# Expert rows read back in two parts, and the end of a streaming encoder layer put in another order

## The reference, cut to what matters

```python
def hier_moe(h, w_group, b_group, w_er, b_er, w_gate, w_up, w_down):
    ...
    p_top, g_top = lax.top_k(jax.nn.softmax(g_logits, -1), 1)
    ...
    e_val, e_top = lax.top_k(e_logits, TOP_E)            # TOP_E = 2 of the group's 8 experts
    gate = jax.nn.softmax(e_val, -1) * p_top
    expert = g_top * EXPERTS_PER_GROUP + e_top            # one of 32
    ...
        hid = jax.nn.silu(xb @ w_gate[e]) * (xb @ w_up[e])   # 1024 -> 256
        return hid @ w_down[e]                               # 256 -> 1024
    ...
    out = out.astype(jnp.float32) * buf_w[:, None]
    return jnp.zeros((n, d), jnp.float32).at[buf_tok].add(out)

x = x + hier_moe(rmsnorm(x, g_ffn), ...)
y = rmsnorm(x, g_final)
```

## Time and profile before

| what | value |
|---|---|
| time, median of 3 executions | 1193.99 us (1193.21 to 1194.16) |
| the profiled execution's own time | 1192.71 us |
| its span, first to last instruction | 1190.9 us |
| mean granted TensorE clock | 0.992 |
| PE, DVE, ACT, POOL busy | 94%, 51%, 40%, 15% |
| HBM read and written | 177.85 MB and 30.18 MB |

### The profile page before, as it was taken

The page is one execution under the profiler, slowest core; times in us unless marked ns, Lnnn a source line. Parts: engine busy times, 40 slices in busy tenths (PEclk is TensorE's granted clock), DMA queues, the critical chain, the costliest instruction groups (busy, mean ns, idle before and its releaser), DMA issues.

```text
span 1190.9 us, 20137 instructions
## 1 busy us (share of the span) xinstructions
PE 1119.6 (94%) x7781; PEld 802.2 (67%) x7781; DVE 607.6 (51%) x1613; ACT 480.7 (40%) x1037; POOL 176.4 (15%) x268
## 2 busy tenths in 40 slices
PE   6997799999999899999999899999899999999986
PEld 5984478787878798898988678887733333333352
DVE  6528978888888785733333373355411112121126
ACT  6437668687878524244343462221011111111113
POOL 1320023434343300000000000000112121111002
PEclk9999999999999999999999999999999999999998
DMA  8343140402112043142442444202899999999748
GB/s 288 48 88 64 36 102 1 106 11 69 48 33 59 19 118 114 53 128 72 119 121 80 151 168 171 92 37 75 338 382 383 420 418 420 418 420 415 304 176 337
DMA packets 127251, 205.44 MB, mean 173 GB/s; under 512 B 15109, under 2 KB 100389, under 8 KB 114869
## 3 DMA queue, kind: packets, MB, share of 16 engines
q1 hardware_dynamic: 114868, 177.63, 42.2%
q0 software_dynamic: 10560, 21.02, 5.2%
q10 hardware_dynamic: 1728, 5.51, 1.2%
HBM read 177.85 MB, written 30.18 MB: 175 GB/s over the span
## 4 chain that ended last, share of the span: by engine, by line
PE 75%; DVE 12%; DMA 4%; ACT 4%; issue 3%; SPq 1%; POOL 0%; DVEq 0%; POOLq 0%; ACTq 0%
PE psum L2512 14%; PE psum L2527 7%; PE psum L2231 5%; PE psum L2233 5%; PE psum L2232 5%; DVE place L1471 3%; PE psum L2382 3%; PE psum L2203 3%; PE psum L2384 2%; PE psum L2383 2%; PE psum L2204 2%; PE psum L2205 2%; PE psum L2313 2%; PE psum L2479 2%; DMA place<-expert_out 2%
## 5 line engine op out<-in xcount | busy, mean ns | idle before, releaser
L2512 PE MATMUL psum<-place,place 128*32 128x512 f32 x1536 | 169.8, 594 | 1.7 <-issue 0.9
L1123 ACT ACTIVATE place<-place,place 128x768 uint8<-128x768 f32 (+3 forms) x128 | 125.5, 983 | 6.7 <-DVE place L1502 6.7
L2231 PE MATMUL psum<-place,place 128*128 128x512 f32 x288 | 121.9, 423 | 2.4 <-DVE place L1459 2.4
L2512 PEld LDWEIGHTS psum<-place,place 128*32 128x32 f32 x1536 | 48.7, 110 | 104.0 <-issue 101.4
L2233 PE MATMUL psum<-place,place 128*128 128x512 f32 x288 | 113.4, 394 | 0.0
L2232 PE MATMUL psum<-place,place 128*128 128x512 f32 x288 | 112.5, 391 | 0.0
L1917 DVE TENSOR_TENSOR place<-psum,place 128x256 f32<-128x256 f32 x24 | 10.2, 427 | 154.6 <-ACT place L1303 154.6
L2527 PE MATMUL psum<-place,place 128*32 128x512 f32 x768 | 86.9, 592 | 0.7 <-DVE place L1911 0.7
L2203 PE MATMUL psum<-place,place 128*128 128x256 f32 x288 | 85.6, 297 | 1.6 <-ACT place L1145 1.6
L2204 PE MATMUL psum<-place,place 128*128 128x256 f32 x288 | 82.1, 285 | 0.0
L2205 PE MATMUL psum<-place,place 128*128 128x256 f32 x288 | 82.0, 285 | 0.0
(11 more groups left out here) (306 smaller groups left out, 2435.9 us busy)
## 6 DMA issues: line engine op xcount, KB each, us to landing
place<-in_w_gate SPq DMA_DIRECT2D x32, 1024.0 KB
place<-in_w_up SPq DMA_DIRECT2D x32, 1024.0 KB
place<-in_w_down SPq DMA_DIRECT2D x32, 1024.0 KB
place<-in_w_in SPq DMA_DIRECT2D x28, 512.0 KB, 6.7
place<-expert_out SPq DMA_DIRECT2D x9, 1024.0 KB, 14.4
place<-in_cache_attn_k SPq DMA_DIRECT2D x32, 256.0 KB, 3.4
place<-in_cache_attn_v SPq DMA_DIRECT2D x32, 256.0 KB, 3.2
place<-in_x_prompt SPq DMA_DIRECT2D x3, 1536.0 KB, 9.4
```

Source lines behind the costliest of these rows:

```text
L1123: last = nc.scalar.activation(reached[j], score[j], ACT.Sign, bias=pivot.bitcast(F32)[:, j:j + 1], scale=-1.0, accum_out=minus[:, j - BY_A ...
L2231: nc.tensor.matmul(bank(4 + b), hT_hi[:, k, rows], hi, start=k == 0, stop=False)
L2512: last = nc.tensor.matmul(bank(b % 2)[rows], xT[b % 2][:, k, rows], w_gu[expert_of(b, q) % NSLOT][:, :, k, :], start=k == 0, stop=k == KD - 1)
```

## The change

The last three blocks (CUT = 21 to 23) are taken out of the table that the tiles are loaded from.

- Blocks 0 to 20 are scattered to expert_out as before, blocks 21 to 23 to a second table late_rows_out. SyncE fills both with zeros during retention heads 0 and 1, so that a row that a table lacks reads as zero.
- SyncE loads y_in[t] once the scatters of blocks 0 to 20 have landed, into weight buffers of experts 27 to 29 that are free by then. Some loads also wait for a block that read the buffer.
- A frame with a pick in blocks 21 to 23 is computed anew in the order of slots. Each late block has 128 slots. For them GpSimd gathers the residual rows (x1_dram, which SyncE writes), the pick's gates and the block of its other pick (pick_table, 2304 rows of 3 numbers, written by ScalarE's queue in block 0), and the other pick's result row, from the early or the late table (other_rows). VectorE adds the own pick straight from the block's rows in SBUF and the other pick. These are "tiles" 9 to 11 of the end; their rows are stored to y_p by index, after all stores of tiles 0 to 7. The sample tile is loaded by late rows on top of its early ones instead.
- Two of VectorE's tiles are summed ahead of the hidden product of block 23 and the others between its last steps. The tiles of TensorE are now 5, 6, 7 and 8. ScalarE makes the diagonal matrices in iteration 22 and takes three sums of squares before the last eviction. The roots are taken in eight groups. The stores of tiles are issued by SyncE. The idle transposes are gone.
- 12 tiles are squared, rooted, scaled and stored in place of 9.

```diff
-AWAKE_FIRST, AWAKE_ROUTE, AWAKE_LAST = (6, 9, 5), (6, 9, 9, 9, 30), 40
-ON_PE, LAST_ORDER = (1, 3, 5, 7), (0, 2, 1, 4, 3, 6, 5, 7, 8)
+CUT = NMAIN - 3
+LATE_BLOCKS = range(CUT, NMAIN)
+NLATE = len(LATE_BLOCKS)
+ON_PE = (5, 6, 7, TP)
+ON_DVE = tuple(t for t in range(T) if t not in ON_PE)
+AWAKE_FIRST, AWAKE_ROUTE = (6, 9, 5), (6, 9, 9, 9, 30)
...
+        late_rows_out = nc.dram_tensor("late_expert_out", (2 * NTOK, D), F32).ap()
...
+        x1_dram = nc.dram_tensor("residual_frames", (NTOK, D), F32).ap()
+        pick_table = nc.dram_tensor("picks", (2 * NTOK, 3), F32).ap()
...
+        LAST = list(ON_DVE) + list(ON_PE[:-1]) + LATE_ROWS + [TP]
+        ROOTS = [(0, 2), (2, 3), (3, 5), (5, 6), (6, 7), (7, 8), (8, 8 + NLATE), (8 + NLATE, 9 + NLATE)]
...
+                    empty = late_rows_out if h else expert_out
+                    sp.dma_start(empty.rearrange("(n p) d -> p n d", p=P), zeros.unsqueeze(1).broadcast_to([P, 2 * T, D])).then_inc(zeroed[0], 16)
...
+                sp.dma_start(x1_dram[t * P:(t + 1) * P, :], x1[:, t, :]).then_inc(x1_out, 16)
...
+            sp.wait_ge(y_out[0], 16 * ((CUT + 1) // 2))
+            sp.wait_ge(y_out[1], 16 * (CUT // 2))
             for t in range(T):
+                if t == 3:
+                    sp.wait_ge(gu_ps, last_block(28) + 1)
+                if t == 5:
+                    sp.wait_ge(dn_ps, last_block(28) + 1)
+                if t == 6:
+                    sp.wait_ge(gu_ps, last_block(29) + 1)
+                if t == TP:
+                    sp.wait_ge(dn_ps, last_block(29) + 1)
                 sp.dma_start(y_in[t], expert_out.rearrange("(j t p) d -> t p j d", j=2, p=P)[t]).then_inc(y_loaded(t)[0], 16)
+            y_p, y_s = o_["y_p"].rearrange("a s d -> (a s) d"), o_["y_s"].rearrange("b s d -> (b s) d")
+            for x, t in enumerate(LAST[:TP]):
+                sp.wait_ge(out_done, x + 1)
+                sp.dma_start(y_p[t * P:(t + 1) * P, :], out_rows[t]).then_inc(y7_out[x % 3], 16)
+            sp.wait_ge(out_done, T + NLATE)
+            sp.dma_start(y_s, out_rows[TP]).then_inc(y_s_out[0], 16)
...
+            pool.memset(zeros, 0.0).then_inc(pool_set, 1)
...
+            def late_frames(n):
+                b = CUT + n
+                if n == 2:
+                    pool.wait_ge(h2tr_ps, T + NMAIN)
+                pool.indirect_dma_start(late_x1[n], None, x1_dram, bass.IndirectOffsetOnAxis(ap=block_frames[:, b:b + 1], axis=0),
+                                        bounds_check=NTOK - 1, oob_is_err=False).then_inc(late_x1_in[0], 16)
+
+            def picks_of(n):
+                b = CUT + n
+                pool.indirect_dma_start(late_picks[:, n, :], None, pick_table, bass.IndirectOffsetOnAxis(ap=block_rows[:, b:b + 1], axis=0),
+                                        bounds_check=2 * NTOK - 1, oob_is_err=False).then_inc(late_picks_in[0], 16)
+
+            def other_picks(n, late):
+                pool.indirect_dma_start(other_rows[n], None, late_rows_out if late else expert_out,
+                                        bass.IndirectOffsetOnAxis(ap=late_others[:, late, n:n + 1], axis=0),
+                                        bounds_check=2 * NTOK - 1, oob_is_err=False).then_inc(others_in[0], 16)
...
+            def root(g):
+                start, end = ROOTS[g]
+                pool.wait_ge(ssq_done, 2 * T + end)
+                pool.tensor_scalar(ssq7[:, start:end], ssq7[:, start:end], 1.0 / D, EPS, ALU.mult, ALU.add).then_inc(ms_done, 1)
+                pool.wait_ge(ms_done, 2 * T + g + 1)
+                pool.tensor_tensor(rstd7[:, start:end], ssq7[:, start:end], half.broadcast_to([P, end - start]), ALU.pow).then_inc(rstd_done, 1)
...
+                if b == NMAIN:
+                    pool.wait_ge(*picks_out)
+                    pool.wait_ge(*late_cleared)
+                    pool.wait_ge(x1_out, 16 * RH + 16 * T)
+                    for n in range(NLATE):
+                        picks_of(n)
+                    late_frames(0)
+                    late_frames(1)
+                if b == NMAIN + 2:
+                    for n in range(2, NLATE):
+                        late_frames(n)
+                if b == NMAIN + 3:
+                    pool.wait_ge(*others_ready)
+                    pool.wait_ge(gu_ps, NMAIN)
+                    pool.wait_ge(y_out[0], 16 * ((CUT + 1) // 2))
+                    pool.wait_ge(y_out[1], 16 * (CUT // 2))
+                    for n in range(NLATE):
+                        other_picks(n, 0)
+                    root(0)
+                if b == NMAIN + 4:
+                    root(1)
                 if b >= 5:
                     scatter(b - 5)
...
+            root(2)
+            for m in range(2):
+                pool.wait_ge(y_out[m], 16 * (NMAIN // 2))
+            pool.wait_ge(others_in[0], 48 + 16 * NLATE)
+            for n in range(NLATE):
+                other_picks(n, 1)
+            root(3)
+            pool.wait_ge(*y_loaded(TP))
+            for j in range(2):
+                pool.indirect_dma_start(y_in[TP][:, j, :], None, late_rows_out, bass.IndirectOffsetOnAxis(ap=sample_late[:, j:j + 1], axis=0),
+                                        bounds_check=2 * NTOK - 1, oob_is_err=False).then_inc(sample_in[0], 16)
+            for g in range(4, len(ROOTS)):
+                root(g)
+            for m in range(3):
+                pool.wait_ge(y7_out[m], 16 * ((TP + 2 - m) // 3))
+            y_p = o_["y_p"].rearrange("a s d -> (a s) d")
+            for n in range(NLATE):
+                pool.wait_ge(out_done, TP + n + 1)
+                pool.indirect_dma_start(y_p, bass.IndirectOffsetOnAxis(ap=late_write[:, n:n + 1], axis=0), out_rows[T + n], None,
+                                        bounds_check=SEQ - 1, oob_is_err=False).then_inc(late_out[0], 16)
...
+                if b == 0:
+                    act.dma_start(pick_table.rearrange("(j t p) m -> p (j t) m", j=2, p=P), pick_values.rearrange("p j t m -> p (j t) m")).then_inc(picks_out[0], 16)
+                if b == NMAIN - 2:
+                    act.wait_ge(gu_ps, NMAIN - 1)
...
+                            nc.scalar.activation(gate_diagonal[n][j], ident, ACT.Copy, scale=gates[:, j, t:t + 1]).then_inc(mix_hi_done, 1)
+                if b == NMAIN - 1:
+                    act.wait_ge(gu_ps, NMAIN)
+                    square(0)
+                    square(1)
...
+            square(2)
             rows_out(NMAIN - 1)
...
+            def own_pick(n):
+                if n == 0:
+                    v.wait_ge(*late_x1_in)
+                    v.wait_ge(y_act, NMAIN)
+                    v.wait_ge(y_dve, NMAIN)
+                nc.vector.scalar_tensor_tensor(late_x1[n], y_of(CUT + n), late_picks[:, n, 0:1], late_x1[n], ALU.mult, ALU.add).then_inc(own_done[0], 1)
+
+            def other_pick(n):
+                if n == 0:
+                    v.wait_ge(*others_in)
+                v.wait_ge(own_done[0], own_done[1] + n + 1)
+                nc.vector.scalar_tensor_tensor(late_x1[n], other_rows[n], late_picks[:, n, 1:2], late_x1[n], ALU.mult, ALU.add).then_inc(x2_done, 1)
+
...
+                if b + 1 == NMAIN:
+                    for t in (0, 1):
+                        for j in range(2):
+                            pick_sum(t, j)
                 hidden(b)
+                if b + 1 == NMAIN:
+                    pick_sum(2, 0)
                 if b >= 1:
                     rows_out(b - 1)
                 if b + 2 < NMAIN:
                     rows_second(b + 2)
                 hidden_turned(b)
+                if b == 1:
+                    late_index()
+                if b == CUT:
+                    late_index_all()
+            pick_sum(2, 1)
+            pick_sum(3, 0)
             rows_out(NMAIN - 1)
+            pick_sum(3, 1)
+            pick_sum(4, 0)
+            pick_sum(4, 1)
...
+            for x in range(3):
+                scaled_rows(x)
+            for n in range(NLATE):
+                own_pick(n)
+            for x in range(3, 6):
+                scaled_rows(x)
+            for n in range(NLATE):
+                other_pick(n)
+            for x in range(6, T + NLATE):
+                scaled_rows(x)
...
             pe.wait_ge(mix_hi_done, T + 2 * len(ON_PE))
-            pe.wait_ge(y_act, NMAIN)
-            pe.wait_ge(y_dve, NMAIN)
-            stay_awake(AWAKE_LAST, idle)
             for n, t in enumerate(ON_PE):
-                pe.wait_ge(*y_loaded(t))
+                pe.wait_ge(*(sample_in if t == TP else y_loaded(t)))
+                if n == 3:
```

More of the change, by code:

```diff
@@ L625, in y_loaded, with summed @@
             return (y7_in[t], 16) if t < T - RING else (cache_in[t - T + RING], 16 * (LATE_VALUES // RING) * AH + 16)
-        def x2_after(x):
-            return sum(0 if t in ON_PE else 2 for t in LAST_ORDER[:x + 1])
+        LATE_ROWS = [T + n for n in range(NLATE)]
+        LAST = list(ON_DVE) + list(ON_PE[:-1]) + LATE_ROWS + [TP]
```

(18 more changed lines are left out.)

149 lines of the change are left out of this document (98 added, 51 removed).

## The result

The changed kernel takes 1195.73 us (median of 20 executions, 1192.47 to 1197.7), the kernel before, on the same chips, 1193.42 us (20 executions). The ratio is 1.0016, 95% interval [1.0009, 1.0023]: 0.16% slower, where 0.7% less was forecast. This is inside the 0.2% bound that the prediction set, but outside its range (1178 to 1192), and the sign is the other one. The profiled execution took 1196.09 us, its span is 1194.3; before, 1192.71 and 1190.9, with TensorE at a mean clock of 0.992, now 0.984.

A forecast was written before the change was run, and what follows sets the result against it. It saw 46 us behind the experts' last matmul, and an expert stage limited by weight loads. Tail end 1180.5 plus 2.0 of stalls gave a span of 1182.5 against 1190.9; median forecast 1185.5, range 1178 to 1192.

The forecast's parts named there:

- The last store goes from issue to the end in 5.1 us: Program end: 4 us taken behind VectorE's queue, to 1180.5, with late row stores ending about when the last store does.
- Zero fills, memset, residual writes: 0.: Early traffic: fills in idle DMA time, memset in a pause, eight residual writes beside normed rows; cost 0.
- The pick table: 2.6 us of DMA (bounds 1.3 to 15): Block 0: 2304 writes of 12 bytes cost 2.6 us, twice the 1.3 us from 16-byte reads; upper end 15.
- Stalls: 2.0 us more.: Weight waits at blocks 18 and 21: 1.1 us from table and residual tile, 0.9 from gathers; 2.0 in all (0 to 16).
- Block 20's rows in at 1123, loads 0 and 1 in by 1129.: Ahead of hidden(23): scatter issued at 1118.67 lands about 1123, loads by 1129; early sums cost 0 with 1.6 us cover.
- VectorE's tail: 27.2 us of work and 3 to 4 of waiting.: Behind the last eviction: 11.7 + 15.5 us of work, 3 to 4 us standing for late other picks; ends at 1176.5.
- clock 0.5 at tile 8's matmuls: Sign in the tail: TensorE at half clock after waiting for sample rows, tile 8 taking 7 us instead of 5.15.
- if the stretch before 1071 is longer than now by more than 1 us: Sign for the time ahead of block 18: growth beyond 1 us would make the prediction wrong.
- the likeliest case's range: Tail from 1177.5 to 1185 with stalls of 0 to 5: median 1180.5 to 1191; chance 0.58.
- B: Rival, chance 0.09: later weights pushed back at blocks 18 and 21; 16 us of stalls, median 1199.6, deciding from 10.4 us.
- C: Rival, chance 0.11: changed tail serialises behind GpSimd loads and frame stores; roots 5 us late, end 1187.5, median 1190.5.
- D: Rival: loads wait for y_in[8], free only after down(22) at 1139.8; only the ninth load; inside C's price, no own chance.

The follow-up runs named there:

- Experiment 1: The changed kernel without its three indexed stores of late rows, so part of the output is missing: 1190.69 us, ratio 0.9982 to the kernel before.
- 2: The kernel before plus one indexed GpSimd store of 128 rows to a spare table at the end, waited for by GpSimd: 1198.84 us, ratio 1.0048.
- 3: The kernel before plus one plain GpSimd store of 128 rows to a spare table at the end, waited for by GpSimd: 1198.88 us, ratio 1.0042.
- 4: The kernel before plus one indexed GpSimd store of 128 rows at the end, its landing waited for by SyncE: 1195.47 us, ratio 1.0016.
- 9: The changed kernel with the wait for its late row stores moved from GpSimd to SyncE: 1194.21 us, ratio 1.0005 to the kernel before.
- experiment 5: The kernel before plus the change's early traffic alone (zero fills, memset, residual writes, table of 2304 12-byte pieces, content unused): 1194.44 us, ratio 1.0010.
- experiment 7: The changed kernel with the pick table written as 128 pieces of 216 bytes, plus six short VectorE steps: 1193.30 us, ratio 0.9998 to the kernel before.
- experiment 8: The changed kernel without its three late gathers of the other pick, so some frames get only one: 1194.99 us, ratio 1.0012 to the kernel before.
- 6: The changed kernel with the pick table written four times, three of them to spare tables: 1216.34 us, ratio 1.0192 to the kernel before.
- 10: The changed kernel with the 216-byte-piece pick table and SyncE waiting for the late row stores: 1191.32 us, ratio 0.9987 to the kernel before.

## Why the prediction was wrong, point by point

*The step that failed: "The last store goes from issue to the end in 5.1 us ...; the three late row stores wait for all frame stores and end at about the same time. I take 4 us."* It was 13.0 us from the last scaled tile. The 5.1 us were read off a store from ScalarE's queue, and I carried them to GpSimd's, of which the trace of before has no case at the end. They were a transfer on an unseen path, and needed bounds from both sides. Experiment 1 takes 6.7 us of the 9.0 away; experiments 2 and 3 add 5.7 and 5.0 us to a kernel that has nothing else of the change; 4 and 9 give a part back (3.8 and 1.3 us; in the trace 3.2 and 2.7). So GpSimd's late stores are the cause, and its own wait for them is most of the price in the kernel before and a part of it in the changed one: there, with SyncE waiting, 5.4 us still stand between landing and end, against 2.9 in experiment 1, and why a late store of GpSimd costs that even when it doesn't wait stays open. What is left over the forecast's 4 us in experiment 1 is 2.3: 4 itself was 1.2 below what the earlier trace rows showed.

*Zero fills, memset, residual writes: 0.* Nothing speaks against it; experiment 5 holds them and the table together to 1.2 us.

*The pick table: 2.6 us of DMA (bounds 1.3 to 15).* About right: the stretches of experiment 7 give some 3.0 us of the stream against 128 pieces, and 2.1 us of it show in the time. The value was taken at twice the nearest row, the 16-byte reads of the earlier trace rows; the estimate is 21 ns a piece against 9 for that read. The Trainium skill's rule on transfers under 512 bytes ("DMA: Bandwidth & Descriptors", Specifications) pointed the right way. Experiment 7 has pieces of 216 bytes, also under 512, and with the same bytes in 18 times fewer of them most of the cost is gone: the number of pieces counts here.

*Stalls: 2.0 us more.* The pauses are 0.44 + 0.69 + 1.63 = 2.76 us against 0.95, so 1.8 more, and 1.6 more by the means of four traces of either kind (2.6 against 1.0: the kernel before and experiments 2, 3 and 4 have 0.95, 1.36, 0.33 and 1.37). Right in size. The place is not the forecast's: two of the three pauses stand at blocks 9 and 12 (966.40 and 1002.46), and not at 18 and 21.

*Block 20's rows in at 1123, loads 0 and 1 in by 1129.* The scatter was issued at 1122.36 and took 8.0 us to land; the loads were issued at 1130.41. The DMA share is 0.96 over 1124 to 1128, with weights and residual gathers beside it, and 0.45 over 1128 to 1132, which is what the late start left unused. TensorE then waited 3.89 us for its first tile, and VectorE began its first sum at 1135.51 in place of 1129.95. The cover of 1.6 us was gone with that: the fourth sum ends at 1141.0, just as hidden(23) begins at 1140.92. Against the last eviction, which is 3.77 us later than before, this product is 4.14 us later, so at most 0.4 us was lost there. The first sum was 5.6 us late and the last eviction hardly felt it. Whether the later loads cost something further down the tail, no run separates.

*VectorE's tail: 27.2 us of work and 3 to 4 of waiting.* 32.2 us, with waits of 3.12, 2.94 and 0.44: 6.5 where 4 was taken, the excess at a root and not at the picks. Right in kind, 1.0 us too low. Both waits have one source. The scatter of block 23 was issued at 1150.88 and took 7.8 us to land, so GpSimd issued the late other picks from 1159.53 on, where 1153 to 1156 was forecast; and root 3, whose sum of squares was ready at 1160.37, stood behind the third of them until 1164.58.

*"clock 0.5 at tile 8's matmuls".* Wrong: it ran at 1.00 over 1168 to 1176, behind a pause of 1.65 us; the slow stretch came at tile 5, behind 3.89 us (0.63 over 1152 to 1156). It cost VectorE nothing, since the root of tile 5 waited for GpSimd longer than for the squares.

*"The prediction is wrong ... if the stretch before 1071 is longer than now by more than 1 us."* It is: the turning of gathered rows ahead of block 18 begins at 1071.91 in place of 1068.92, 3.0 us later. 1.1 us of this are the two pauses for weights named above, which the forecast had put at block 18. 1.4 us are there by the first expert blocks (870.28 against 868.89), and they begin at a place that the change doesn't touch: behind a pause at the end of retention TensorE runs at half clock for longer. The last 0.5 us weren't followed. In the kernel before and in the changed one (granted clock third from the end):
```profile
406.00:412.00 6.00, 5.91 (x47) 5.59 (x49) 3.82 (x12) 0.40 (x3) 2.29 (x3) 0.72 0.05 14
```
```profile
406.00:412.00 6.00, 5.68 (x26) 5.68 (x27) 4.04 (x12) 0.27 (x2) 2.51 (x3) 0.50 0.05 14
```
The profile of experiment 3, which is the kernel before up to 1185 us, has 0.50 there as well; that of experiment 8 has 1.00. So it belongs to the execution and not to the change. It makes up 1.4 of the 1.75 us by which the last eviction was later than forecast. How much of it the medians hold stays open.

*The sums.* Two are off: by its own terms the likeliest case's range ends at 1185 + 5 + 3.1 = 1193.1 and not at 1191, and the 9.4 us of table that B needs to reach 10.4 of stalls are 65 ns a piece, not 70. Neither decides anything.

*The rivals.* B (the expert stage starves) occurs in kind only: 1.8 us of stalls against the 10.4 from which it decides, since the table cost some 3 us and not 15. C is nearest: its words were "row stores behind all frame stores", and it was priced at 5 us for the roots, of which 3.1 came, and at nothing for the end. D did not occur.

## What to carry to other kernels

A program's end has a price of its own, and it depends on which engine issues the last transfer and waits for it: keep the last stores off GpSimd's queue, or let another engine wait for them, before shortening what lies ahead (only the second was tried here). A small table of many pieces costs more than its bytes say, so lay it out as one piece per partition (2.1 us here), and look at the queue of the engine that issues it as well as at the DMA engines before putting a price on it. And a duration read off one queue does not hold for another; where the trace has no case, bound the step from both sides like any other.

## What was not expected of the hardware

- The end of the program came 10.0 to 11.3 us after the end of GpSimd's last issue where GpSimd waited for the landing (six kernels: the changed one, 2, 3, 6, 7, 8), and 6.8 to 7.85 where SyncE did (4, 9, 10); 4.5 to 5.9 us after the last issue where GpSimd issued nothing late (the kernel before, 1, 5). Counted from the last landing it is 6.7 to 8.0, 3.5 to 5.4, and 2.1 to 2.9 us.
- Three tables of 2304 writes of 12 bytes, issued behind a first one, held ScalarE's queue for 33.5 us; the first issue took 0.39. With one table the DMA engines moved 107 GB/s for 4 us at a share of 0.95.
- A scatter of 128 rows (0.52 MB) took 8.0 us to land beside weights, 7.8 us in the tail beside the loads, and 11.1 us in the median of the changed kernel's 24.
